# The MLP up projection of a two-block network with the high and low halves of the activations moved together, 512 columns per matmul

## The chip, the cores and the metric

One core of one Trainium2 chip. The metric is device microseconds of one launch, the median of several runs.

## The reference

A network of three layers on 256 tokens of width 1,024, all in float32. The first layer has sparse attention, forgetting attention and gated embeddings, the other two a mixer with cross attention, an output projection and an MLP. What the change touches is the MLP of the last two layers, cut to its lines:

```python
D_FF = 4 * D_MODEL          # 4,096

u = rms_norm(x, g_mlp[i])
x = x + jnp.square(jax.nn.relu(u @ w_ff1[i])) @ w_ff2[i]
```

`u` is 256 x 1,024, `w_ff1` 1,024 x 4,096 and `w_ff2` 4,096 x 1,024. So each MLP has an up projection, a squared relu, and a down projection that is added to `x`.

## The kernel before, in words

**Numbers.** Every float32 factor of a large product is split into a high part (rounded to the type float32r) and a low part (what is left, in the same type). A product then takes three matmuls that add up in PSUM: high by high, high by low, low by high. ScalarE makes the high part of a piece of weights (a copy with rounding from `raw` to `w_hi`, L677, in the loops of the MLP L954) and VectorE the low part (a subtraction into `w_lo`, L1024, in the loops L1349).

**Units.** Weights come in units of 128 x 2,048: four blocks of 128 rows by 512 columns. SyncE loads a unit into one of two landing buffers `raw` (L458), after waiting for the subtraction (`lo_ready`) of the unit that lay there. Split units lie in a ring of four slots; ScalarE and VectorE split three units ahead of TensorE. TensorE raises `unit_used` when it has used up a unit, and ScalarE waits for that before it writes a slot again. Every engine runs the same sequence of units, written out by hand, and signals the others by semaphores.

**The activations.** `u` is transposed on TensorE (L1506), and ScalarE and VectorE read the transposes from PSUM into `a_hi` (L693, L694) and `a_lo` (L1036), each 128 x 8 x 256: 8 blocks k of the width, 256 tokens.

**The MLP.** The hidden width of 4,096 is cut into FF = 8 chunks of 512. A chunk needs two up units (each four of the eight blocks k) and two down units (each 512 of the 1,024 output columns).

- Up (`up`, L1730 to L1744). The weights are stationary, 128 x 128 blocks (k, f) with f one of four parts of the chunk; the activations move, 256 columns. The result of part f is hidden-transposed, 128 x 256, in the first half of bank 4 + f. For each (k, f) there are three matmuls (L1742): w_hi with a_hi, w_hi with a_lo, w_lo with a_hi. A unit has 48 matmuls, a chunk 96.
- Eviction. ScalarE applies four relus, one per bank, from PSUM to `hidden` (L932, in the tile `tok`), each of which raises `ff_relu`. VectorE waits for all four and squares `hidden` in place (L1331). ScalarE rounds it to `b_hi` (L938), VectorE subtracts to `b_lo` (L1335) and raises `ff_lo`.
- Down (`product`, L1434 to L1450). The hidden values are stationary, the weights move, 512 columns: 24 matmuls for a unit, 48 for a chunk (L1446), which add up over all chunks in banks 0 to 3. The last unit of all goes by token tiles (L1460).

**The order on TensorE** (`mlp`, `chunk`). up(0), then for each chunk i: up(i+1), a wait for `ff_lo` of chunk i, down(i). Before the first matmul into bank f, up(i+1) waits until `ff_relu` says that this bank of chunk i was read (L1740). So chunk i+1 is evicted during down(i), except for chunk 0, whose eviction has no down product to lie beside: up(1) follows up(0) directly.

**The order on ScalarE in a chunk** (`chunk`, L946): split a unit, `hidden_hi`; split a unit, `hidden_relu` of the next chunk; split, split. `hidden_relu` waits for `unit_used` of the second up unit, `hidden_hi` also for the down product that read `b_hi` before. **On VectorE** (L1342): subtract for a unit, `hidden_lo`; subtract, `hidden_square`; subtract, subtract. What is queued behind a waiting instruction on an engine waits with it.

Of the kernel before, what the change touches and what calls it, by code (L numbers as in the profile page):

```python
# [18 lines left out]
ALU = mybir.AluOpType  # L19
ACT = mybir.ActivationFunctionType  # L20
AX = mybir.AxisListType
F32 = mybir.dt.float32
F32R = mybir.dt.float32r
BF16 = mybir.dt.bfloat16

P = 128
# [24 lines left out]
FF = 8  # L51
# [170 lines left out]
def build(nc, a, out):  # L222
    with ExitStack() as ctx:
        def sb(name, shape, dt=F32):
            return ctx.enter_context(nc.sbuf_tensor(name, shape, dt))

        def sem(name):
            return ctx.enter_context(nc.semaphore(name))
# [5 lines left out]
        tok = sb("tok", [P, NT, D])  # L234
        a_hi = sb("a_hi", [P, KT, S], F32R)
        a_lo = sb("a_lo", [P, KT, S], F32R)
        b_hi = sb("b_hi", [P, KT, S], F32R)
# [30 lines left out]

        bank = [ctx.enter_context(nc.psum_tensor(f"bank{i}", [P, 512], F32)) for i in range(8)]

        b_t, b_io, b_s, b_v, b_tr = bank[2], bank[3], bank[4:6], bank[7], bank[6:8]
        b_hid = bank[4:8]

        def group_bank(g):
# [60 lines left out]
        d_ready, y_ready, y_made = sem("d_ready"), sem("y_ready"), sem("y_made")  # L335
        ff_relu, ff_sq, ff_hi, ff_lo, rstd_sq = sem("ff_relu"), sem("ff_sq"), sem("ff_hi"), sem("ff_lo"), sem("rstd_sq")
        head_sum, ident_made = sem("head_sum"), sem("ident_made")
# [333 lines left out]
        def _(act):  # L671
# [253 lines left out]
            def mlp(base, lay, r, gx, gain):  # L925
                def hidden_relu(used, free):

                    act.wait_ge(unit_used, used)
                    if free is not None:
                        act.wait_ge(ff_lo, free)  # L930
                    for f in range(4):
                        act.activation(hidden[:, f, :], b_hid[f][:, 0:S], ACT.Relu).then_inc(ff_relu, 1)  # L932

# [9 lines left out]
                unit(base + 1)  # L943
                hidden_relu(base + 3, lay * FF if lay else None)

                def chunk(i, peeled):  # L946
                    for r_ in range(4):
# [10 lines left out]
                        if r_ == 1:  # L958
                            hidden_relu(i * 4 + (base + 5), i + (lay * FF + 1))
                with act.Fori(0, FF - 2) as i:  # L960
# [51 lines left out]
        def _(dve):  # L1012
# [315 lines left out]
            def mlp(base, lay, gx, gain):  # L1328
                def hidden_square(n):
                    dve.wait_ge(ff_relu, n * 4)  # L1330
                    dve.tensor_tensor(hidden, hidden, hidden, ALU.mult).then_inc(ff_sq, 1)  # L1331

# [100 lines left out]
        def _(pe):  # L1433
# [295 lines left out]
            def mlp(base, lay, gx, x_before, after):  # L1729
                def up(u, half_, slot, mid=(), read=None):  # L1730


                    pe.wait_ge(lo_ready, u + 1)
                    for k in range(4):
                        if k in mid:
                            mid[k]()
                        for f in range(4):
                            w = slice(k * CB + f * P, k * CB + f * P + P)
                            if read is not None and k == 0:
                                pe.wait_ge(ff_relu, read + (f + 1))  # L1740
                            for q, (wa, xa) in enumerate(((w_hi, a_hi), (w_hi, a_lo), (w_lo, a_hi))):
                                ins = pe.matmul(b_hid[f][:, 0:S], wa[:, slot, w], xa[:, 4 * half_ + k, :],  # L1742
                                                start=half_ + k + q == 0, stop=half_ == 1 and k == 3 and q == 2)
                    ins.then_inc(unit_used, 1)  # L1744
# [6 lines left out]
                def chunk(i, first, last):  # L1751

                    s = [(base + 2 + r) % RING for r in range(4)]
                    if not last:
                        up(i * 4 + (base + 2), 0, s[0], read=i * 4 + 4 * lay * FF)
                        up(i * 4 + (base + 3), 1, s[1])
# [116 lines left out]
```

## Time and profile before

| | |
|---|---|
| three runs | 882.53, 882.95, 885.64 us; median 882.95 |
| profiled execution, first to last instruction | 888.5 us (the page states no other time of it) |
| TensorE busy | 867.2 us, 4,726 matmuls |
| weight loads busy | 725.7 us, 4,726 loads |
| VectorE busy | 512.3 us |
| ScalarE busy | 420.8 us |
| mean granted TensorE clock | 0.987 of full speed |

PE is TensorE's matmuls and PEld its weight loads, which lie beside them; DVE is VectorE, ACT ScalarE, POOL GpSimd, SPq the queue of SyncE. L1742 is line 1742 of the kernel. Matmuls are pipelined: the duration shown of one (283 ns for 256 columns) is longer than the distance to the next, so their cost is read from the starts, or from the length of a stretch divided by its matmuls. In square brackets behind an instruction stand the idle time of its engine before it and what ended it. The MLP of the first of the two layers lies at 389 to 571 us of the span, that of the second at 704 to 885 us.

### The profile page before, as it was taken

The page shows a single profiled execution, that of the slowest core. Times are in us where ns is not written, and L with a number is a line of the kernel's source. Part 1 is how long each engine was busy: PE and PEld are TensorE (multiplying, and loading weights), DVE is VectorE, ACT ScalarE, POOL GpSimd, SP SyncE. Part 2 cuts the span into 40 slices and gives each one's busy share as a digit, 9 for nine tenths or more (in the row PEclk, how much of TensorE's full clock was granted, in tenths as well). Part 3 has the DMA queues.
Part 4 walks back from the last instruction along what each step waited for, and adds up shares of the span by engine and source line. Part 5 has one row for each costly group of instructions (what it writes and reads, how often), then busy time and mean ns, then how long its engine had stood idle before and what let it go on. Part 6 is the DMA issues. An engine that isn't in the chain of part 4 may idle for free. (4 is left out here: it accounts for less than half of the span.)

```text
span 888.5 us, 12248 instructions
## 1 busy us (share of the span) xinstructions
PE 867.2 (98%) x4726; PEld 725.7 (82%) x4726; DVE 512.3 (58%) x646; ACT 420.8 (47%) x613; POOL 132.3 (15%) x156
## 2 busy tenths in 40 slices
PE   7999999999999998999999999999999999999998
PEld 6996887777887775899999999877756899999996
DVE  5555576556767765455555555576764565555552
ACT  6445455454365554354444444445445454444440
POOL 3500010000003143002000000068940010000000
PEclk9998999999999998999999999999979999999999
DMA  8941234345655373146555555553310555555541
GB/s 321 299 142 37 68 123 142 98 140 174 206 200 186 133 243 122 42 149 201 183 189 188 187 188 189 188 190 99 139 48 18 172 190 190 189 189 189 188 142 48
DMA packets 76056, 140.59 MB, mean 158 GB/s; under 512 B 2728, under 2 KB 22384, under 8 KB 76016
## 3 DMA queue, kind: packets, MB, share of 16 engines
q1 hardware_dynamic: 73984, 134.03, 45.0%
q0 software_dynamic: 1872, 5.94, 2.1%
q8 instruction: 27, 0.44, 0.2%
q14 instruction: 13, 0.11, 0.0%
q10 hardware_dynamic: 160, 0.07, 0.0%
HBM read 138.99 MB, written 1.05 MB: 158 GB/s over the span
## 5 line engine op out<-in xcount | busy, mean ns | idle before, releaser
L1024 DVE TENSOR_TENSOR w_lo<-raw,w_hi 128x2048 fp32r<-128x2048 f32 (+2 forms) x69 | 157.7, 2287 | 76.3 <-ACT w_hi L677 75.6
L677 ACT ACTIVATE w_hi<-raw 128x2048 fp32r<-128x2048 f32 (+2 forms) x69 | 129.9, 1883 | 72.6 <-PE bank L1446 46.9
L1349 DVE TENSOR_TENSOR w_lo<-raw,w_hi 128x2048 fp32r<-128x2048 f32 x48 | 110.1, 2294 | 91.6 <-ACT w_hi L954 91.6
L1446 PE MATMUL bank<-w_hi,a_hi 128*128 128x512 f32 (+2 forms) x376 | 148.4, 395 | 0.4 <-PE bank L1446 0.4
L1446 PE MATMUL bank<-w_hi,b_hi 128*128 128x512 f32 x376 | 148.3, 394 | 0.3 <-DVE b_lo L1032 0.2
L1446 PE MATMUL bank<-w_lo,b_hi 128*128 128x512 f32 x376 | 146.6, 390 | 0.0
L1446 PE MATMUL bank<-w_hi,b_lo 128*128 128x512 f32 x376 | 146.5, 390 | 0.0
L1742 PE MATMUL bank<-a_hi,w_hi 128*128 128x256 f32 x512 | 145.3, 284 | 1.1 <-ACT tok L932 1.1
L1742 PE MATMUL bank<-a_lo,w_hi 128*128 128x256 f32 x512 | 144.9, 283 | 0.0
L1742 PE MATMUL bank<-a_hi,w_lo 128*128 128x256 f32 x512 | 144.9, 283 | 0.0
L1446 PE MATMUL bank<-w_lo,a_hi 128*128 128x512 f32 (+2 forms) x376 | 143.3, 381 | 0.0
L1446 PE MATMUL bank<-w_hi,a_lo 128*128 128x512 f32 (+2 forms) x376 | 143.3, 381 | 0.0
L954 ACT ACTIVATE w_hi<-raw 128x2048 fp32r<-128x2048 f32 x48 | 92.2, 1922 | 98.5 <-PE bank L1446 61.2
L1742 PEld LDWEIGHTS bank<-a_hi,w_hi 128*128 128x128 f32 x512 | 98.2, 192 | 2.0 <-DVE w_lo L1024 1.5
L1742 PEld LDWEIGHTS bank<-a_lo,w_hi 128*128 128x128 f32 x512 | 98.2, 192 | 0.5
L1742 PEld LDWEIGHTS bank<-a_hi,w_lo 128*128 128x128 f32 x512 | 98.2, 192 | 0.0
L1446 PEld LDWEIGHTS bank<-w_hi,a_hi 128*128 128x128 f32 x376 | 71.7, 191 | 15.0 <-issue 4.6
L1446 PEld LDWEIGHTS bank<-w_hi,b_hi 128*128 128x128 f32 x376 | 70.6, 188 | 15.1 <-issue 1.0
L1446 PEld LDWEIGHTS bank<-w_hi,b_lo 128*128 128x128 f32 x376 | 70.6, 188 | 15.1
L1446 PEld LDWEIGHTS bank<-w_lo,b_hi 128*128 128x128 f32 x376 | 70.7, 188 | 13.7
L1446 PEld LDWEIGHTS bank<-w_hi,a_lo 128*128 128x128 f32 x376 | 71.6, 190 | 11.7
L1446 PEld LDWEIGHTS bank<-w_lo,a_hi 128*128 128x128 f32 x376 | 71.8, 191 | 9.7
(213 smaller groups left out, 972.8 us busy)
## 6 DMA issues: line engine op xcount, KB each, us to landing
raw<-in_w_ff SPq DMA_DIRECT2D x64, 1024.0 KB, 5.1
raw<-in_w_out SPq DMA_DIRECT2D x12, 1024.0 KB, 5.0
raw<-in_w_in_moba SPq DMA_DIRECT2D x20, 512.0 KB, 4.4
raw<-in_w_merge SPq DMA_DIRECT2D x8, 1024.0 KB, 5.0
raw<-in_w_in SPq DMA_DIRECT2D x6, 880.0 KB, 7.5
m<-in_w_in SPq DMA_DIRECT2D x6, 880.0 KB, 6.9
raw<-in_w_mem_kv SPq DMA_DIRECT2D x4, 1024.0 KB, 5.2
raw<-in_w_ple_gate SPq DMA_DIRECT2D x4, 1024.0 KB, 5.0
```

Of the source, the lines that this page charges most:

```text
L677: act.activation(w_hi[:, slot, 0:n], landing[land][:, 0:n], ACT.Copy).then_inc(hi_ready, 1)
L954: act.activation(w_hi[:, (base + c) % RING, :], raw[:, (base + c) % RAW, :], ACT.Copy)\
L1024: dve.tensor_tensor(w_lo[:, v % RING, 0:n], landing[land_slot(v)][:, 0:n], w_hi[:, v % RING, 0:n].bitcast(F32), ALU.subtract).then_inc(lo_ ...
L1349: dve.tensor_tensor(w_lo[:, (base + c) % RING, :], raw[:, (base + c) % RAW, :], w_hi[:, (base + c) % RING, :].bitcast(F32), ALU.subtract). ...
L1446: ins = pe.matmul(banks[t][:, 0:n], xa[:, k0 + k, ts], wa[:, slot, w], start=first and k == 0 and q == 0, stop=last and k == kts - 1 and q ...
L1742: ins = pe.matmul(b_hid[f][:, 0:S], wa[:, slot, w], xa[:, 4 * half_ + k, :], start=half_ + k + q == 0, stop=half_ == 1 and k == 3 and q == 2)
```

## The change

`a_hi` and `a_lo` become two halves of one tile `a_both`, so that for a block k the 256 high and the 256 low columns lie side by side. Banks 4 to 7 become one PSUM tensor of four banks. For each (k, f) the up projection moves all 512 columns past w_hi in one matmul: the first half of the bank gets w_hi by a_hi, the second w_hi by a_lo. A second matmul of 256 columns adds w_lo by a_hi to the first half. So there are two matmuls in place of three, 64 for a chunk in place of 96. In the last block k the short one comes first, so that the long one closes the group.

The eviction sums the two halves: ScalarE copies the second halves of all four banks to `hidden` in one instruction of 1,024 columns, in place of four relus (`ff_part` replaces `ff_relu`); VectorE adds the first halves of the banks to it (1,024 columns, raises `ff_sum`), and then takes max(h, 0) * h in one instruction in place of the square. TensorE waits once for `ff_sum`, ahead of the first matmul of an up stretch, in place of four times for `ff_relu`.

```diff
--- before.py
+++ after.py
@@ -232,8 +232,8 @@
         w_lo = sb("w_lo", [P, RING, UNIT], F32R)
         x = sb("x", [P, NT, D])
         tok = sb("tok", [P, NT, D])
-        a_hi = sb("a_hi", [P, KT, S], F32R)
-        a_lo = sb("a_lo", [P, KT, S], F32R)
+        a_both = sb("a_both", [P, KT, 2, S], F32R)
+        a_hi, a_lo = a_both[:, :, 0, :], a_both[:, :, 1, :]
         b_hi = sb("b_hi", [P, KT, S], F32R)
         b_lo = sb("b_lo", [P, KT, S], F32R)
         proj = sb("proj", [P, NT * DIN])
@@ -266,10 +266,13 @@
         hstat = sb("hstat", [P, N_NORMED, 2, NT * 4])
         half = sb("half", [P, NT * 4])
 
-        bank = [ctx.enter_context(nc.psum_tensor(f"bank{i}", [P, 512], F32)) for i in range(8)]
+        low = [ctx.enter_context(nc.psum_tensor(f"bank{i}", [P, 512], F32)) for i in range(4)]
+        high = ctx.enter_context(nc.psum_tensor("bank4", [P, 4, 512], F32))
+        bank = [b[:, :] for b in low] + [high[:, i, :] for i in range(4)]
 
         b_t, b_io, b_s, b_v, b_tr = bank[2], bank[3], bank[4:6], bank[7], bank[6:8]
         b_hid = bank[4:8]
+        hid_lo, hid_hi = high[:, :, 0:S], high[:, :, S:2 * S]
 
         def group_bank(g):
 
@@ -333,7 +336,8 @@
         merge_sig, merged, x_post, z_made = sem("merge_sig"), sem("merged"), sem("x_post"), sem("z_made")
         ple_block, d_copied_a, d_copied_v = sem("ple_block"), sem("d_copied_a"), sem("d_copied_v")
         d_ready, y_ready, y_made = sem("d_ready"), sem("y_ready"), sem("y_made")
-        ff_relu, ff_sq, ff_hi, ff_lo, rstd_sq = sem("ff_relu"), sem("ff_sq"), sem("ff_hi"), sem("ff_lo"), sem("rstd_sq")
+        ff_part, ff_sum = sem("ff_part"), sem("ff_sum")
+        ff_sq, ff_hi, ff_lo, rstd_sq = sem("ff_sq"), sem("ff_hi"), sem("ff_lo"), sem("rstd_sq")
         head_sum, ident_made = sem("head_sum"), sem("ident_made")
         act_chain, vec_chain, pool_chain = sem("act_chain"), sem("vec_chain"), sem("pool_chain")
 
@@ -923,13 +927,12 @@
             evac(B_KV0)
 
             def mlp(base, lay, r, gx, gain):
-                def hidden_relu(used, free):
+                def hidden_part(used, free):
 
                     act.wait_ge(unit_used, used)
                     if free is not None:
                         act.wait_ge(ff_lo, free)
-                    for f in range(4):
-                        act.activation(hidden[:, f, :], b_hid[f][:, 0:S], ACT.Relu).then_inc(ff_relu, 1)
+                    act.activation(hidden, hid_hi, ACT.Copy).then_inc(ff_part, 1)
 
                 def hidden_hi(n, used, k=0):
 
@@ -941,7 +944,7 @@
                 groups(gx, 2, a_hi, gain)
                 x_squares(r, X_OUT0 + 2 if lay == 0 else X_OUT1 + 2, m_hi)
                 unit(base + 1)
-                hidden_relu(base + 3, lay * FF if lay else None)
+                hidden_part(base + 3, lay * FF if lay else None)
 
                 def chunk(i, peeled):
                     for r_ in range(4):
@@ -956,7 +959,7 @@
                         if r_ == 0:
                             hidden_hi(i + (lay * FF + 1), i * 4 + (base + 3))
                         if r_ == 1:
-                            hidden_relu(i * 4 + (base + 5), i + (lay * FF + 1))
+                            hidden_part(i * 4 + (base + 5), i + (lay * FF + 1))
                 with act.Fori(0, FF - 2) as i:
                     chunk(i, False)
                 chunk(FF - 2, True)
@@ -1327,8 +1330,10 @@
 
             def mlp(base, lay, gx, gain):
                 def hidden_square(n):
-                    dve.wait_ge(ff_relu, n * 4)
-                    dve.tensor_tensor(hidden, hidden, hidden, ALU.mult).then_inc(ff_sq, 1)
+                    dve.wait_ge(ff_part, n)
+                    dve.tensor_tensor(hidden, hid_lo, hidden, ALU.add).then_inc(ff_sum, 1)
+                    dve.wait_ge(ff_sum, n)
+                    dve.scalar_tensor_tensor(hidden, hidden, 0.0, hidden, ALU.max, ALU.mult).then_inc(ff_sq, 1)
 
                 def hidden_lo(n, k=0):
                     dve.wait_ge(ff_hi, n)
@@ -1731,16 +1736,20 @@
 
 
                     pe.wait_ge(lo_ready, u + 1)
+                    if read is not None:
+                        pe.wait_ge(ff_sum, read)
                     for k in range(4):
                         if k in mid:
                             mid[k]()
+                        kt = 4 * half_ + k
+                        x_both = a_both[:, kt].rearrange("p q n -> p (q n)")
                         for f in range(4):
                             w = slice(k * CB + f * P, k * CB + f * P + P)
-                            if read is not None and k == 0:
-                                pe.wait_ge(ff_relu, read + (f + 1))
-                            for q, (wa, xa) in enumerate(((w_hi, a_hi), (w_hi, a_lo), (w_lo, a_hi))):
-                                ins = pe.matmul(b_hid[f][:, 0:S], wa[:, slot, w], xa[:, 4 * half_ + k, :],
-                                                start=half_ + k + q == 0, stop=half_ == 1 and k == 3 and q == 2)
+                            if kt < KT - 1:
+                                pe.matmul(b_hid[f], w_hi[:, slot, w], x_both, start=kt == 0, stop=False)
+                            ins = pe.matmul(b_hid[f][:, 0:S], w_lo[:, slot, w], a_hi[:, kt, :], start=False, stop=False)
+                            if kt == KT - 1:
+                                ins = pe.matmul(b_hid[f], w_hi[:, slot, w], x_both, start=False, stop=True)
                     ins.then_inc(unit_used, 1)
                 mids = upper(gx, x, x_half, x_before + 2)
 
@@ -1752,7 +1761,7 @@
 
                     s = [(base + 2 + r) % RING for r in range(4)]
                     if not last:
-                        up(i * 4 + (base + 2), 0, s[0], read=i * 4 + 4 * lay * FF)
+                        up(i * 4 + (base + 2), 0, s[0], read=i + (lay * FF + 1))
                         up(i * 4 + (base + 3), 1, s[1])
                     pe.wait_ge(ff_lo, i + (lay * FF + 1))
                     for c in range(2):
```

## Rows read from the trace of the kernel before

**Rows 1.** The page: busy time of each engine
```profile
PE 867.2 (98%) x4726; PEld 725.7 (82%) x4726; DVE 512.3 (58%) x646; ACT 420.8 (47%) x613; POOL 132.3 (15%) x156
```

**Rows 2.** The chain that ended last, in order of time: start us, us, what
```profile
...
739.84 11.51 PE bank L1742 x96
751.35 10.91 PE bank L1446 x48
...
```

**Rows 3.** One chunk by windows: length; busy PE, PEld, DVE, ACT, POOL; PEclk, DMA, GB/s
```profile
739.84:751.35 11.51, 11.51 (x98) 11.51 (x97) 5.72 (x3) 4.78 (x3) 0.00 (x0) 1.00 0.60 185
751.35:762.26 10.91, 10.91 (x51) 9.02 (x50) 5.81 (x3) 4.93 (x6) 0.00 (x0) 1.00 0.56 191
```

**Rows 4.** Timeline of PE, end of the first up stretch, layer 1: start, us
```profile
...
716.34 0.28 PE L1742 MATMUL bank<-a_hi,w_lo 128*128 128x256 f32 x1
717.18 0.36 PE L1742 MATMUL bank<-a_hi,w_hi 128*128 128x256 f32 x1 [0.56 <-ACT tok L932]
...
```

**Rows 5.** Timeline of PE, the same place in layer 0
```profile
...
402.44 0.36 PE L1742 MATMUL bank<-a_hi,w_hi 128*128 128x256 f32 x1 [0.56 <-ACT tok L932]
...
```

**Rows 6.** The chain of waits inside the first up stretch: transposes, and the wait
```profile
...
707.11 0.44 PE bank L1506 x4
717.05 0.14 issue
...
```

**Rows 7.** Timeline of ACT, then of DVE, at the first eviction of layer 1
```profile
...
716.65 1.21 ACT L932 ACTIVATE tok<-bank 128x256 f32<-128x256 f32 x4 [2.47 <-PE bank L1742]
...
714.21 2.29 DVE L1024 TENSOR_TENSOR w_lo<-raw,w_hi 128x2048 fp32r<-128x2048 f32 x1 [0.81 <-ACT w_hi L677]
717.90 1.23 DVE L1331 TENSOR_TENSOR tok<-tok 128x1024 f32<-128x1024 f32 x1 [1.39 <-ACT tok L932]
...
```

**Rows 8.** Groups of instructions by line and shape, ACT: count, busy us, mean ns, idle before
```profile
...
L932 ACT ACTIVATE tok<-bank 128x256 f32<-128x256 f32 x64 | 19.4, 389 | 58.7 <-PE bank L1742 58.7
L938 ACT ACTIVATE b_hi<-tok 128x1024 fp32r<-128x1024 f32 x16 | 16.7, 1044 | 0.0
L690 ACT ACTIVATE a_hi<-bank 128x512 fp32r<-128x512 f32 x9 | 5.4, 598 | 7.9 <-PE bank L1506 7.8
...
```

**Rows 9.** The same view for DVE
```profile
...
L1331 DVE TENSOR_TENSOR tok<-tok 128x1024 f32<-128x1024 f32 x16 | 19.6, 1226 | 41.4 <-ACT tok L932 41.4
L1032 DVE TENSOR_TENSOR a_lo<-bank,a_hi 128x512 fp32r<-128x512 f32 x9 | 6.2, 689 | 4.4 <-ACT a_hi L690 4.4
L1290 DVE SCALAR_TENSOR_TENSOR m<-m 128x1024 f32<-128x1024 f32 x2 | 2.5, 1226 | 2.4 <-ACT m L897 2.4
...
```

**Rows 10.** Timeline of ACT, then of DVE, from the second eviction on
```profile
...
728.97 1.21 ACT L932 ACTIVATE tok<-bank 128x256 f32<-128x256 f32 x4 [3.85 <-PE bank L1742]
...
730.22 1.23 DVE L1331 TENSOR_TENSOR tok<-tok 128x1024 f32<-128x1024 f32 x1 [2.77 <-ACT tok L932]
732.01 2.29 DVE L1349 TENSOR_TENSOR w_lo<-raw,w_hi 128x2048 fp32r<-128x2048 f32 x1 [0.57 <-ACT w_hi L954]
744.04 1.22 DVE L1335 TENSOR_TENSOR b_lo<-tok,b_hi 128x1024 fp32r<-128x1024 f32 x1
...
```

**Rows 11.** Timeline of DVE in the last chunk of layer 1
```profile
...
868.75 1.22 DVE L1335 TENSOR_TENSOR b_lo<-tok,b_hi 128x1024 fp32r<-128x1024 f32 x1
...
```

**Rows 12.** Timeline of PE: its three longest idle times after the start-up
```profile
...
337.08 0.66 PE L1567 MATMUL bank<-ident,proj 128*128 128x128 f32 x2 [4.63 <-POOL proj L598]
...
596.22 0.41 PE L1567 MATMUL bank<-ident,proj 128*128 128x128 f32 x2 [1.19 <-POOL proj L598]
...
655.25 0.55 PE L1633 MATMUL bank<-ident,prob 128*128 128x128 f32 x3 [1.20 <-DVE prob L1166]
...
```

**Rows 13.** Busy time by window after these idle times; PEclk is the granted clock
```profile
336.00:342.60 6.60, 5.52 (x15) 4.43 (x16) 2.29 (x1) 2.03 (x3) 5.55 (x6) 0.50 0.71 233
596.00:600.00 4.00, 3.78 (x17) 2.86 (x17) 3.10 (x5) 0.80 (x3) 3.67 (x5) 1.00 0.52 174
657.00:662.00 5.00, 5.00 (x16) 2.68 (x15) 1.63 (x8) 2.46 (x10) 0.00 (x0) 0.50 0.02 3
```

## The prediction

> **What bounds the kernel now.** I read the page first. TensorE is busy for 98% of the span, VectorE for 58%, ScalarE for 47% [rows 1]. A busy share alone proves nothing, so I next read the chain that ended last. In one chunk of an MLP it is TensorE alone: 96 up-projection matmuls of 256 columns in 11.51 us, then 48 down-projection matmuls of 512 columns in 10.91 us, and no other engine between them [rows 2]. The windows of the same chunk show the granted clock at 1.00, so the full 2.4 GHz, while DVE works 5.7 of 11.5 us [rows 3]. So in the steady part only TensorE's own issue sets the time. There is one exception in each layer: after the very first up stretch nothing can be put between it and the next one, as the first down product needs the hidden values of a chunk already finished. There TensorE idles until a bank has been read. In layer 1 the last matmul starts at 716.34 and the next at 717.18 [rows 4]; layer 0 shows the same 0.56 us of idle time [rows 5].
>
> **Term 1, the matmuls.** For each weight block (k, f) the change replaces three 256-column matmuls by one of 512 and one of 256. Their spacing is 11.51 / 96 = 119.9 ns and 10.91 / 48 = 227.3 ns [rows 2]. Before: 3 x 119.9 = 359.7 ns. After: 227.3 + 119.9 = 347.2 ns. The columns moved are the same 768; what goes is one of three fixed parts. At 2.4 GHz 256 columns are 106.7 ns and 512 are 213.3 ns, so 13.2 and 14.0 ns of each spacing are not columns. 32 blocks x 8 chunks x 2 layers = 512 blocks, so 512 x 12.5 ns = **6.4 us less**, all on the path. The rounding of the two stretches (0.01 us each) is 0.2 us of this. The 512-column matmul is priced by the down projection, whose moving operand is as long and as contiguous as the new one, but the trace has no alternation of the two sizes. Bounds for the block: above, 359.7 ns, no gain; below, 227.3 + 106.7 = 334.0 ns, the short matmul paying for its columns alone. I take 347.2, since the fixed part has nearly the same size in both stretches.
>
> A rule speaks against this term. The Trainium skill (TensorE: Matmul & The Clock Gate, Back-to-back issue gap) gives warm matmuls N / 2.4 + 2.5 ns apart. By that, each matmul saved is worth 2.5 ns, term 1 is 1.3 us, and the total comes out slower than before. The trace disagrees with the rule by some 11 ns at either size, and I follow the trace.
>
> **Term 2, the first eviction of each layer.** Before, the second up stretch waited bank by bank for ff_relu, so the first of four relus released it. Now one wait on ff_sum covers all four banks, and that needs ScalarE's copy of all high halves and, behind it, VectorE's add. Let N be the moment at which the next matmul would start without a wait. Before, N = 716.34 + 0.12 = 716.46; the first relu starts at 716.65, 0.19 after N [rows 4, 7], takes 0.39, and TensorE starts 0.14 after it [rows 6]: N + 0.72. After: 0.19, then a copy of 1,024 columns. ScalarE takes 389 ns for 256 columns and 598 for 512 [rows 8], so 209 ns per 256 more, 1.02 us for 1,024; the 1,024-column copy from SBUF took 1.04. I take 1.03. Then 0.04 to VectorE (717.86 to 717.90 would be the same step), an add of 1.23 as for 1,024 columns from SBUF [rows 9], and 0.14: N + 2.63. So 1.91 us more in each layer, **3.8 us more** in all. Upper bounds, if a strided read over four banks cost as its parts: copy 4 x 389 = 1.56, add 2 x 689 = 1.38 [rows 8, 9], 0.68 more in each layer, 5.2 in all. Below I see no way under 3.7: both are serial. VectorE is free in time; its weight subtraction ended at 716.50 [rows 7].
>
> **Everything later is covered.** In the steady part the eviction starts when the up stretch ends (728.97) and is needed at 739.84, after a down stretch. Copy to 730.0 (shorter than the four relus' 1.21), add to 731.3: 8.5 us to spare. The added instruction is the second on VectorE: max and square in one, 1.23 us as its like [rows 9], to 732.5. Queued behind it is the weight subtraction that now starts at 732.01 [rows 10], and behind that SP's next load, which waits for the subtraction; both come about 0.5 us later. Their own weights are needed a chunk half later. The hidden low half ends at 744.04 + 1.22 = 745.3, needed at 751.35: 6 us spare. At the end of layer 1 it ends at 869.97 [rows 11] and is needed when 48 matmuls from 863.3 on are over, at 874.2: 4.2 us spare against 1.3 more. ScalarE gets shorter: one copy in place of four relus, 1.03 for 1.21, with the weight roundings queued behind it. If this cover were gone, each of 16 chunks would pay what is over. The new layout of a_hi and a_lo changes only strides between runs of 256; I cost it at nothing, its writers having idle time before them (7.9 us on ScalarE's [rows 8]). No DMA is added or moved.
>
> **Sum.** -6.4 + 3.8 = **-2.6 us**. Each term is a difference inside one profiled execution. The page gives only its span, 888.5 us, and that stands 5.5 us above the median of the three runs, 882.95; I apply the difference to the median: 880.35. With the bounds of the two terms the forecast's own range is -2.9 to -1.0 us, and the three runs shown scatter by -0.4 to +2.7.
>
> **Rival 1, the clock falls at the longer wait (ends slower).** The idle time shown would go from 0.56 to 0.56 + 1.91 = 2.5 us. Two idles of 1.2 us lie far below that [rows 12]: after one, the clock stayed at 1.00, after the other, in a stretch of small matmuls, it fell to 0.50, which is 1.2 GHz. At the idle of 4.63 us it also fell, for the 6.6 us shown [rows 12, 13]. Our 2.5 us lies between, and dense 2.4 GHz work on both sides speaks against a fall. From the point at which 2.5 us is enough, one fall costs up to half of 6.6 us, 3.3: -2.6 + 3.3 = +0.7, 883.6 us; in both layers +4.0, 887.0.
>
> **Rival 2, no cheaper block.** The fixed part of 13 ns isn't paid per matmul when sizes alternate; a block takes 359.7 ns as before. Then only term 2 is left: +3.8, 886.8 us. Against it: two streams with the same fixed part although one has twice the columns. The skill's rule above is nearest to this case.
>
> **Rival 3, weight loads were the limit.** Loads are busy for all of the up stretch, 11.51 of 11.51 us, against 9.02 of 10.91 in the down stretch [rows 3]. If the 119.9 ns are a load's and not the matmul's, and a load can go ahead during the 512-column matmul, the block takes 334.0 ns: 512 x 25.7 = 13.2 us less, -9.4 in all, 873.6 us. Against it: four 128-column transposes with their loads pass in 0.44 us [rows 6], 110 ns each, so a load alone isn't longer than that; and a load would have to run two matmuls ahead.
>
> **How the numbers follow.** Forecast 0.58, rival 1 0.25, rival 2 0.07, rival 3 0.07, the rest (above all an eviction that comes late in every chunk) 0.03. About what a measurement can tell from no change is 0.5%, 4.4 us. Faster by more: rival 3 and 0.03 of the forecast, 0.10. Slower by more: two falls with term 2 at its upper bound 0.03, rival 2 with a longer wait or a fall 0.04, the rest 0.02, so 0.09. Within: 0.81. The range runs from 877.5 (the forecast's best, 880.0, less scatter of the runs and some of the way to rival 3) to 886.0 (past one fall, with scatter); it leaves out rival 3, rival 2 and two falls, under 2 in 10.
>
> **What would show it.** Right: an up stretch of 64 matmuls in 11.1 us; one idle of 2.5 us per layer before the second up stretch, released by VectorE's add; the new add near 1.23 us; the clock at 1.00 in the 7 us after it; no wait of TensorE elsewhere in the MLPs; one weight load fewer per block. Wrong: an up stretch of 11.5 or of 10.7 us (rivals 2 and 3), 0.50 in the clock column after the wait (rival 1), or waits of TensorE for b_lo or ff_sum in each chunk.

## The result, and the profile after

| | before | changed |
|---|---|---|
| median, 20 executions each | 885.83 us | 891.41 us |
| lowest, highest | 882.53, 898.03 | 885.50, 902.09 |
| ratio, 95% interval | 1 | 1.0057, 1.0029 to 1.0085 |
| profiled execution: time, span, mean clock | span 888.5, clock 0.987 | 886.73, 884.9, 0.990 |

The ratio compares undisturbed executions; those more than 1.5% above the fastest of their kernel are left out of it, and with them most of those that lost most to the clock. The change makes the kernel about 0.6% slower; measured twice more (e5_again, e11_third below) the same kernel was 0.3 and 0.2% slower, with intervals that reach 1. Over all 44 executions of it and 121 of before the mean time is 4.0 us longer, 0.45%. The forecast was 880.35 us, 2.6 below the median of three runs then shown; 891.41 lies outside the range of 877.5 to 886.0. The median of before has itself risen by 2.9 us with more executions.

The pages first. The changed kernel has a third less up-projection matmuls, 448 + 512 + 64 in place of 1,536, and still the chain that ended last is TensorE's.

```profile
PE 860.6 (97%) x4214; PEld 697.6 (79%) x4214; DVE 530.5 (60%) x662; ACT 417.8 (47%) x565; POOL 130.6 (15%) x156
...
PE 31%; DVE 1%; POOL 1%; ACT 0%; issue 0%
...
L1749 PE MATMUL bank<-a_both,w_hi 128*128 128x512 f32 x448 | 160.7, 402 | 4.9 <-DVE tok L1334 4.9
...
L935 ACT ACTIVATE tok<-bank 128x1024 f32<-128x1024 f32 x16 | 16.4, 1026 | 56.6 <-PE bank L1752 56.6
L1334 DVE TENSOR_TENSOR tok<-bank,tok 128x1024 f32<-128x1024 f32 x16 | 19.6, 1225 | 36.4 <-ACT tok L935 36.4
```

The copy of 1,024 columns takes 1.03 us and the add 1.23, as in the forecast. Now a steady up stretch by windows, and the stretch right behind the wait of the second MLP (columns as in [rows 3]), both of the changed kernel:

```profile
737.48:748.77 11.29, 11.29 (x65) 9.81 (x64) 5.72 (x3) 4.79 (x3) 0.00 (x0) 1.00 0.61 187
```

```profile
715.39:726.56 11.17, 11.17 (x64) 9.79 (x65) 6.83 (x4) 4.70 (x3) 0.00 (x0) 1.00 0.51 173
```

An up stretch took 11.51 us before [rows 2, 3]. It takes 11.29 now, 0.22 less, and the forecast was 0.40 less. All twelve steady stretches show 11.29 or 11.30. Only the one behind the second wait comes near the forecast, at 11.17 or 11.18.

The waits of the two MLPs, from the timeline of PE in the changed kernel:

```profile
403.46 0.77 PE L1749 MATMUL bank<-a_both,w_hi 128*128 128x512 f32 x1 [2.46 <-DVE tok L1334]
404.02 0.41 PE L1750 MATMUL bank<-a_both,w_lo 128*128 128x256 f32 x1
...
715.39 0.47 PE L1749 MATMUL bank<-a_both,w_hi 128*128 128x512 f32 x1 [2.46 <-DVE tok L1334]
715.70 0.28 PE L1750 MATMUL bank<-a_both,w_lo 128*128 128x256 f32 x1
```

Both are 2.46 us, where 0.56 stood before [rows 4, 5]. But the matmuls behind the first take 0.77 and 0.41 us, behind the second 0.47 and 0.28. The windows tell why; PEclk is the granted clock:

```profile
396.00:403.20 7.20, 4.99 (x29) 4.07 (x27) 5.32 (x3) 3.71 (x4) 6.08 (x14) 1.00 0.52 164
403.20:406.60 3.40, 3.14 (x10) 2.69 (x11) 2.87 (x3) 2.86 (x2) 2.21 (x6) 0.50 0.76 279
406.60:413.00 6.40, 6.40 (x38) 5.55 (x37) 2.35 (x3) 1.92 (x1) 0.00 (x0) 1.00 0.51 164
```

The clock fell from 2.4 to 1.2 GHz at the end of the first wait, for 3.4 us. That is rival 1. In dense work half of 3.4 us is 1.7 us; read from the starts, the stretch behind this wait took 12.78 us and the one behind the second, at full clock, 11.18. The question is whether it explains a loss of 5 us.

**How the executions are compared.** Every execution comes with its span and its mean granted clock c. I call (1 - c) x span the part lost to the clock; where an expectation below speaks of the time without the clock's part, it subtracts this whole. Over all executions of all kernels here a straight line fits with a residual of 1.0 us: time = T + 0.83 x part lost, with a T for each kernel (why the slope is below 1 was not looked into). T is the time at full clock. Both are used below.

### The profile page after: what moved, and what is told of

It is laid out like the page before. It is cut to its first block and busy times, and to the rows that moved or that the text cites. A ratio compares the mean times of both kernels' runs of the same rounds, so it can differ in the third digit from the quotient of the medians.

```text
span 884.9 us, 11144 instructions
## 1 busy us (share of the span) xinstructions
PE 860.6 (97%) x4214; PEld 697.6 (79%) x4214; DVE 530.5 (60%) x662; ACT 417.8 (47%) x565; POOL 130.6 (15%) x156
## 5 line engine op out<-in xcount | busy, mean ns | idle before, releaser
L1451 PE MATMUL bank<-w_hi,a_both 128*128 128x512 f32 (+2 forms) x752 | 239.3, 389 | 0.4 <-PE bank L1451 0.4
L1749 PE MATMUL bank<-a_both,w_hi 128*128 128x512 f32 x448 | 160.7, 402 | 4.9 <-DVE tok L1334 4.9
L1451 PEld LDWEIGHTS bank<-w_hi,a_both 128*128 128x128 f32 x752 | 142.9, 191 | 26.6 <-issue 4.6
L1451 PE MATMUL bank<-w_lo,a_both 128*128 128x512 f32 (+2 forms) x376 | 143.5, 382 | 0.0
L1750 PE MATMUL bank<-a_both,w_lo 128*128 128x256 f32 x512 | 141.6, 282 | 0.0
L1749 PEld LDWEIGHTS bank<-a_both,w_hi 128*128 128x128 f32 x448 | 84.9, 189 | 26.2 <-issue 5.5
L1750 PEld LDWEIGHTS bank<-a_both,w_lo 128*128 128x128 f32 x512 | 97.4, 190 | 1.3
L1451 PEld LDWEIGHTS bank<-w_lo,a_both 128*128 128x128 f32 x376 | 72.0, 192 | 9.6
L1334 DVE TENSOR_TENSOR tok<-bank,tok 128x1024 f32<-128x1024 f32 x16 | 19.6, 1225 | 36.4 <-ACT tok L935 36.4
L792 ACT ACTIVATE probT<-bank 128x384 f32<-128x384 f32 (+1 forms) x36 | 18.5, 514 | 46.1 <-PE bank L1638 45.9
```

The source lines that it names most:

```text
L792: act.activation(probT[:, h % 2, 0:n], b_t[:, 0:n], ACT.Copy).then_inc(pt_copied, 1)
L1334: dve.tensor_tensor(hidden, hid_lo, hidden, ALU.add).then_inc(ff_sum, 1)
L1451: ins = pe.matmul(banks[t][:, 0:n], xa[:, k0 + k, ts], wa[:, slot, w], start=first and k == 0 and q == 0, stop=last and k == kts - 1 and q ...
L1749: pe.matmul(b_hid[f], w_hi[:, slot, w], x_both, start=kt == 0, stop=False)
L1750: ins = pe.matmul(b_hid[f][:, 0:S], w_lo[:, slot, w], a_hi[:, kt, :], start=False, stop=False)
```

## The experiments

Fourteen runs. This table has them all; T has an error of 0.2 us for the first two lines and of 0.3 to 0.4 for the others. The mean part lost has an error of 0.5 us for before, 1.1 for the changed kernel, 1.2 for e1_fill, 0.3 for e8_before_early and 1.3 to 2.8 for the rest. "Large" counts the executions that lost 13 us or more to the clock. The ratio of the second line is that of the 20 executions above.

| kernel | median us | ratio to before, 95% | T | mean part lost | large |
|---|---|---|---|---|---|
| before | 885.9 | | 879.0 | 10.7 | 27 of 121 |
| changed, with e5 and e11 | 891.4 | 1.0057 (1.0029 to 1.0085) | 878.9 | 15.7 | 25 of 44 |
| e1_fill, both waits filled | 885.29 | 0.999 (0.9969 to 1.001) | 878.7 | 9.1 | 1 of 13 |
| e9_fill0, the first filled | 887.33 | 1.0004 (0.9985 to 1.0023) | 878.9 | 11.2 | 2 of 13 |
| e10_fill1, the second filled | 897.09 | 1.0043 (1.0 to 1.0087) | 879.1 | 17.1 | 7 of 12 |
| e13_shift | 887.13 | 1.0004 (0.9971 to 1.0038) | 880.0 | 11.9 | 4 of 13 |
| e4_before_late | 892.34 | 1.0052 (1.0019 to 1.0084) | 883.0 | 13.6 | 4 of 13 |
| e14_before_shift | 889.06 | 1.0001 (0.996 to 1.0041) | 880.8 | 14.4 | 5 of 12 |
| e2_bank | 883.38 | 0.9982 (0.9949 to 1.0015) | 876.2 | 13.0 | 4 of 12 |
| e3_early | 879.85 | 0.9912 (0.9874 to 0.9951) | 874.2 | 11.4 | 3 of 10 |
| e7_early2 | 881.11 | 0.9928 (0.9892 to 0.9963) | 873.5 | 12.2 | 4 of 14 |
| e12_best | 880.50 | 0.9926 (0.9897 to 0.9955) | 873.1 | 10.5 | 1 of 7 |
| e8_before_early | 883.84 | 0.9983 (0.9961 to 1.0005) | 877.5 | 6.9 | 0 of 12 |
| e6_grouped | 887.18 | 1.0013 (0.9986 to 1.004) | 877.9 | 11.9 | 3 of 12 |

The first two lines alone answer most of it. T is the same: 878.9 against 879.0. What the matmuls gain, the waits take. The changed kernel loses 5.0 us more to the clock (error 1.2), and 0.83 x 5.0 = 4.1 us is the difference of the mean times, 891.9 and 887.9.

**Fill the waits.**

```diff
                 up(base + 1, 1, (base + 1) % RING, mids[1])
+                for _ in range(10):
+                    pe.matmul(bank[3], a_both[:, 0, 0, 0:P], a_both[:, 0].rearrange("p q n -> p (q n)"), start=True, stop=True)
```

> The changed kernel, with ten 512-column matmuls into an unused bank placed in the wait between the first and the second up stretch of each layer (10 x 0.227 = 2.3 us of the 2.5 us idle). Theory A (the longer idle makes the clock fall, in layer 0 at this wait in the trace of after, and that is where the loss is): no stretch at clock 0.50 in the 10 us behind this place in either layer, second up stretch 11.2 to 11.3 us, and the time comes back to that of before, ratio 0.998 to 1.002. Theory B (the falls of the clock are chance and have nothing to do with the wait; the loss is the wait itself and dearer blocks): nothing changes against the changed kernel, ratio about 1.006.

Idle is down to 0.18 us and the second stretch starts no earlier:

```profile
400.49 2.45 PE L1760 MATMUL bank<-a_both 128*128 128x512 f32 x10
403.12 0.47 PE L1749 MATMUL bank<-a_both,w_hi 128*128 128x512 f32 x1 [0.18 <-DVE tok L1334]
```

The windows of the 10 us behind it, and behind the second wait of the same kernel, are at clock 1.00:

```profile
403.00:413.00 10.00, 9.88 (x56) 8.60 (x57) 6.87 (x4) 4.72 (x3) 2.11 (x6) 1.00 0.58 198
725.00:735.00 10.00, 9.82 (x56) 8.48 (x56) 6.73 (x5) 4.78 (x3) 0.00 (x0) 1.00 0.58 199
```

T does not move (878.7), the part lost falls from 15.7 to 9.1 us, and the ratio is 0.999, as theory A had it. Useless work in the wait makes the kernel faster. So the idle time of TensorE, and not the length of the wait, is what costs beyond T.

The two stretches behind the filled waits were not both 11.2 to 11.3 us long, as expected:

```profile
403.12:414.48 11.36, 11.36 (x64) 9.89 (x65) 7.05 (x4) 4.60 (x3) 1.99 (x5) 1.00 0.50 172
725.34:736.52 11.18, 11.18 (x65) 9.80 (x65) 6.84 (x4) 4.61 (x3) 0.00 (x0) 1.00 0.49 170
```

Both come after 0.18 us of idle, in the same order of matmuls at the same clock. So the short stretch of 11.17 us in the changed kernel isn't owed to the length of the idle before it.

**The wait alone, in the kernel before.**

```diff
+                    if read is not None:
+                        pe.wait_ge(ff_sq, read)
...
-                            if read is not None and k == 0:
-                                pe.wait_ge(ff_relu, read + (f + 1))
...
-                        up(i * 4 + (base + 2), 0, s[0], read=i * 4 + 4 * lay * FF)
+                        up(i * 4 + (base + 2), 0, s[0], read=i + (lay * FF + 1))
```

> The kernel before with one edit: an up stretch waits for the square of the chunk (ff_sq) and not for the relu of the bank. All matmuls are as before; the first wait of each layer gets as long as in the changed kernel (0.19 + 1.21 + 0.04 + 1.23 + 0.14 = 2.8 us, 2.1 more than before), elsewhere it is covered by the down stretch. Theory A: +4.2 us of wait, and the clock falls to 0.50 behind it in some executions for 1.7 to 3.4 us more each: ratio 1.006 to 1.011. Theory B: +4.2 us alone, ratio 1.0048, clock at 1.00 behind both waits.

T is 4.0 us above that of before, where 4.2 was expected. The idle is 2.65 us at both places, and the profile shows the clock at 0.50 behind it at 404.3 and again at 728.6:

```profile
402.90:404.30 1.40, 1.40 (x12) 1.40 (x13) 0.00 (x0) 1.40 (x2) 1.40 (x8) 1.00 1.03 399
404.30:407.70 3.40, 3.40 (x18) 3.40 (x18) 3.35 (x2) 0.97 (x2) 0.20 (x1) 0.50 0.15 56
407.70:413.00 5.30, 5.30 (x46) 5.30 (x46) 0.78 (x2) 1.91 (x1) 0.00 (x0) 1.00 0.63 198
...
728.60:732.00 3.40, 3.40 (x17) 3.40 (x17) 1.92 (x1) 2.40 (x2) 0.00 (x0) 0.50 0.52 202
```

The fall needs none of the new matmuls. At the first wait it came 1.4 us after TensorE had begun to work again, so it need not lie in the idle time but can follow it. The part lost is 2.9 us more than before, with an error of 2.0. The ratio, 1.0052, is just below what was expected of theory A (1.006 to 1.011) and cannot be told from B by itself; the two falls in the trace decide for A.

**The changed kernel again.** Twice, once as the reference of the fills of one wait.

> The changed kernel itself once more, beside the kernels of this call. So far, time less what the clock took ((1 - mean clock) x span, for each execution) is 877.2 us for before and 876.1 for the changed kernel, while the part lost to the clock is 8.8 us (median) before and 15.1 after. Theory A: this holds again; the time without the clock's part is 0.5 to 1.5 us below that of before, the part lost is 3 to 6 us larger, and a profile shows a fall behind one or both of the 2.5 us waits. Theory B (the clock's part was the chance of that session): the clock's part is within 1.5 us of that of before, and the ratio is 0.998 to 1.000.

It measured 890.33 us, ratio 1.0029 (0.9996 to 1.0062), part lost 15.9 us. The fall at 403.1 us is there again, none behind the second wait.

> The changed kernel a third time, as the reference for the two beside it in the same call: time without the clock's part as before (within 0.5 us), mean loss 14 to 17 us, large losses in a third to two thirds of the executions; one more profile, in which the fall behind the first wait should be there, and either one behind the second or a long one near 650 us.

It measured 892.68 us, ratio 1.0024 (0.999 to 1.0059), part lost 15.5 us, large in 7 of 12. Its profiled execution lost 17.4 us, a large loss. It has three falls to look at: behind the first wait, in the attention of the last mixer, and behind the second wait.

```profile
402.10:405.50 3.40, 3.40 (x11) 2.92 (x12) 2.89 (x2) 2.60 (x2) 1.92 (x5) 0.50 0.67 249
...
654.70:668.40 13.70, 13.61 (x41) 7.40 (x41) 5.21 (x21) 5.43 (x19) 1.37 (x2) 0.50 0.00 0
...
719.50:722.90 3.40, 3.12 (x9) 2.67 (x10) 2.64 (x3) 2.86 (x2) 0.00 (x0) 0.50 0.71 267
```

**Which wait?** Two kernels with the filling matmuls in one MLP only; e9_fill0 has the condition shown, e10_fill1 has `U_FF1` in it.

```diff
-                for _ in range(10):
+                for _ in range(10 if base == U_FF0 else 0):
```

> The changed kernel with the ten filling matmuls in the wait of the first MLP only (at 400 us); the wait of the second (at 713 us) stays idle. So far the part lost to the clock is 15.8 us (mean of 32 executions) in the changed kernel, 9.1 with both waits filled, 10.4 before, and losses of 13 us and more are in 18 of 32 executions of the changed kernel, 1 of 13 filled. Theory A1 (each wait only costs its own fall, 1.7 us apiece): mean loss 13 to 14, large losses as often as in the changed kernel. Theory A2 (the fall at the first wait also makes the falls at 580 to 685 us longer, by what it does to the timing ahead of them): mean loss 9.5 to 12 here, large losses in at most 3 of 12.

> The same with the second wait filled and the first idle. Theory A1: mean loss 13 to 14. Theory A2: as in the changed kernel less the second wait's own fall, mean 14 to 16, large losses in a third to a half of the executions, and a profile shows the fall at 403 us.

The two kernels do the same work, T 878.9 and 879.1, and both leave one wait of 2.46 us idle. With the first filled the part lost is 11.2 us and large in 2 of 13; with the second filled 17.1 and large in 7 of 12. This speaks for A2, in two small samples: an idle first wait brings more than its own fall. Before lost 10.4 to 11.9 us on average on each of four chips, so the chip doesn't explain the difference.

What is a large loss made of? Six profiled executions lost more than 20 us (e1, e2, e4, e7, e9, e13), and each has one stretch of 30.7 or 34.1 us at 1.2 GHz in the small matmuls of the attention, from 651 to 657 us on. In the profile of e9_fill0, one of its two executions with such a loss, it is this:

```profile
653.90:688.00 34.10, 34.10 (x103) 18.22 (x102) 12.37 (x50) 12.75 (x44) 1.14 (x2) 0.50 0.00 0
```

The kernel before has a shorter one at the same place, 10.2 us in its profile with 11.9 us lost. But 13 us are also passed without a long stretch, and more easily by a kernel with falls at its waits: e11_third reached 17.4 us with 13.7 us there and two falls of 3.4, and the profile of e6_grouped 13.7 us with none there, but falls at both waits and one at 599 us. So "large" counts two things. At 20 us the changed kernel has 12 of 44 executions and before 21 of 121, which chance can give. If the line for before is lowered by two falls, from 13 to 9.6 us, it has 39 of 121 against the 25 of 44, and chance hardly gives that. e9_fill0 and e10_fill1 keep their 2 of 13 and 7 of 12 at 20 us.

In e10_fill1 the profile showed no fall at 403 us after the same 2.46 us, so the fall doesn't come each time, against what was expected of that profile.

**Does the shift do it?** A fall at the first wait moves everything behind it by 1.7 us. Two kernels make that shift without a fall: 17 filling matmuls in place of 10 in the first wait, and eleven in the kernel before. The first edit is that of e13_shift, on top of e1_fill, the second that of e14_before_shift, at the same place of the kernel before.

```diff
-                for _ in range(10):
+                for _ in range(17 if base == U_FF0 else 10):
...
+                for _ in range(11 if base == U_FF0 else 0):
+                    pe.matmul(bank[3][:, :], a_hi[:, 0, 0:P], a_hi[:, 0:2, :].rearrange("p k n -> p (k n)"), start=True, stop=True)
```

> The changed kernel with both first waits filled, the first by 17 matmuls in place of 10: 7 x 0.227 = 1.6 us more at full clock, about what a fall of the clock there costs, and no fall. Time without the clock's part: 0.3 us of the 1.6 is still the wait, so 1.2 us above e1_fill. If the shift of everything behind by 1.6 us makes the later falls long, losses of 13 us and more come in a third to two thirds of the executions and the mean loss is 13 to 17 us. If it does not, they come in at most 3 of 12, mean 9 to 11.

> The kernel before with eleven 512-column matmuls into an unused bank after the first up stretch of the first MLP: 2.5 us, of which 0.7 cover the wait there, so +1.8 us without the clock's part. If the shift makes the later falls long: mean loss 13 to 17 us, ratio to before above 1.005. If not: mean loss 9 to 11 as before, ratio 1.001 to 1.003.

T rose by 1.3 and 1.8 us, as expected. Large losses came in 4 of 13 and 5 of 12, 9 of 25 together. That lies between the 27 of 121 of before and the 32 of 56 of the changed kernel and e10_fill1 together. It decides nothing. Nor is the idle first wait the whole rule: e4_before_late and e6_grouped have it too and show 4 of 13 and 3 of 12. All kernels with it make 39 of 81, those with the wait filled or at most 1.02 us (before and its shift among them, e1, e2, e3, e7, e8, e9, e12, e13) 51 of 227. At 20 us these are 23 of 81 and 44 of 227, which no longer tells them apart.

**Where the matmuls' gain went.** The blocks (k, f) in another order: all four 512-column matmuls of a row k, then all four of 256.

```diff
-                        for f in range(4):
...
-                            if kt < KT - 1:
-                                pe.matmul(b_hid[f], w_hi[:, slot, w], x_both, start=kt == 0, stop=False)
-                            ins = pe.matmul(b_hid[f][:, 0:S], w_lo[:, slot, w], a_hi[:, kt, :], start=False, stop=False)
+                        if kt < KT - 1:
+                            for f in range(4):
+                                pe.matmul(b_hid[f], w_hi[:, slot, ws[f]], x_both, start=kt == 0, stop=False)
+                        for f in range(4):
+                            ins = pe.matmul(b_hid[f][:, 0:S], w_lo[:, slot, ws[f]], a_hi[:, kt, :], start=False, stop=False)
...
```

> The changed kernel with the matmuls of a block row k in another order: four of 512 columns, then four of 256, so that sizes alternate once in eight matmuls. Steady up stretches of the changed kernel take 11.29 us and not the 11.11 of the forecast. If the alternation of sizes costs the missing 5.6 ns per block, the stretch is 11.11 to 11.15 us here and the time without the clock's part 2 to 3 us lower than that of the changed kernel. If it is something else (a 512-column matmul of this shape is dearer than one of the down projection), it stays at 11.29. Waits and the clock's part as in the changed kernel either way.

The steady stretch by windows:

```profile
428.30:439.51 11.21, 11.21 (x66) 9.83 (x65) 5.72 (x3) 4.78 (x3) 0.00 (x0) 1.00 0.58 189
```

11.21 us, 0.08 of the missing 0.18. T is 1.0 lower (error 0.4), not 2 to 3. So the alternation of sizes is a part of it and not all. The expectation was right in kind and too large.

**Take the wait away.** First the eviction bank by bank, as before the change.

```diff
-                    act.activation(hidden, hid_hi, ACT.Copy).then_inc(ff_part, 1)
+                    for f in range(4):
+                        act.activation(hidden[:, f, :], hid_hi[:, f, :], ACT.Copy).then_inc(ff_part, 1)
...
-                    dve.wait_ge(ff_part, n)
-                    dve.tensor_tensor(hidden, hid_lo, hidden, ALU.add).then_inc(ff_sum, 1)
-                    dve.wait_ge(ff_sum, n)
+                    for f in range(4):
+                        dve.wait_ge(ff_part, n * 4 + (f - 3))
+                        dve.tensor_tensor(hidden[:, f, :], hid_lo[:, f, :], hidden[:, f, :], ALU.add).then_inc(ff_sum, 1)
+                    dve.wait_ge(ff_sum, n * 4)
...
-                    if read is not None:
-                        pe.wait_ge(ff_sum, read)
...
+                            if read is not None and k == 0:
+                                pe.wait_ge(ff_sum, read * 4 + (f - 3))
```

> The changed kernel with the eviction bank by bank: four copies of 256 columns, four adds of 256, TensorE waits for ff_sum of one bank. The wait should end 0.19 + 0.39 + 0.04 + 0.42 + 0.14 = 1.2 us after the next matmul could start, in place of 2.7. Theory A: 2 x 1.5 = 3 us less from the wait, and no fall of the clock there, so ratio to before 0.995 to 0.999. Theory B: only the 3 us less than the changed kernel, ratio about 1.0025.

The idle is 1.02 us, T 876.2: 2.7 us below the changed kernel, for 3 expected. The median part lost is 7.9 us and its profile has no fall at either wait. Its mean is 13.0, from four executions of large loss, so these come without a wait of 2.46 us too.

Then, on top of e2_bank, the second up unit in an order that finishes bank 0 early; ScalarE copies a bank as soon as `ff_bank` says that it is finished:

```diff
+                    for k in range(2 if half_ else 4):
...
+                        for f in range(4):
+                            ins = block(k, f)
+                    if half_:
...
+                        for f in range(4):
+                            block(2, f)
+                            ins = block(3, f)
+                            if f < 3:
+                                ins.then_inc(ff_bank, 1)
```

> As the one before, and the second up unit finishes bank by bank (blocks k = 2 and 3 of bank f together), so that bank 0 can be evicted 2 us before the stretch ends. No idle of TensorE at the first eviction (before: 0.56 us). Theory A and B both: 12 to 14 steady chunks x 0.22 us less plus twice the 0.7 us that before waits, so 4 to 5 us less than before at the same clock. A: ratio 0.993 to 0.997. B: the clock falls as in the changed kernel by chance, ratio 0.997 to 1.002.

0.9912: faster than before beyond the interval. T is 4.8 us under it, as expected, though an idle of 0.52 us remained, since VectorE's weight subtraction lay ahead of the adds. So the next kernel takes the adds first:

```diff
                 unit(base)
-                unit(base + 1)
                 hidden_square(lay * FF + 1)
+                unit(base + 1)
```

> The third kernel of the first call (bank-wise eviction, second up unit finished bank by bank) with one more edit: VectorE does the first adds of a layer before its second weight subtraction, which held them up to 399.87 there. The first adds then start near 398.3, and the 0.52 us idle before the second up stretch goes in both layers: 1.0 to 1.5 us less than e3_early without the clock's part (872.3), so 871; ratio to before 0.989 to 0.993 by either theory.

The 0.52 us of idle are gone. T is 0.7 lower with an error of 0.5, where 1.0 to 1.5 was expected, and the ratio cannot be told from that of e3_early. To see how much of this is the order and how much the wide matmuls, the kernel before got the same order, with its relus:

> The kernel before, its matmuls of 256 columns kept, with the second up unit finished bank by bank so that relus run during the stretch. What e3_early gains over before is then split: the idle of 0.56 us goes here too, 2 x 0.7 = 1.4 us less than before without the clock's part (877.2), so 875.8. If this kernel came as low as e3_early (872.3), the 512-column matmuls would have no part in that gain; by the traces they have 3.5 us of it.

T 877.5, 1.5 under before (1.4 expected), ratio 0.9983. It lost least of all to the clock, 6.9 us with no large loss in 12; but the three kernels with this order and the wide matmuls have 8 large losses in 31, so this isn't shown to be the order's doing. Of the 5.5 us of e7_early2 this leaves 4.0 for the wide matmuls, where 12 steady and 4 first stretches of 0.22 to 0.25 us give 3.5 to 4.0. At last both orders together:

> A version meant to beat both: e7_early2 (bank-wise eviction, second up unit finished bank by bank, first adds ahead of the weight subtraction) with the order of e6_grouped where a block row runs over all banks. e7_early2 stands 5.5 us under before without the clock's part; the grouped rows cover 6 of 8 block rows of a stretch whose gain was 0.08 us, so 12 x 0.06 = 0.7 us more. Ratio to before 0.990 to 0.994, no idle over 0.2 us at the first eviction.

Timeline of PE behind the first eviction of the second MLP, and a steady stretch by windows, of e12_best:

```profile
708.37 0.50 PE L1751 MATMUL bank<-a_both,w_hi 128*128 128x512 f32 x1 [0.20 <-DVE tok L1339]
```

```profile
730.06:741.24 11.18, 11.18 (x65) 9.79 (x65) 7.04 (x5) 5.94 (x6) 0.00 (x0) 1.00 0.69 228
```

0.9926 (0.9897 to 0.9955), 5.9 us under before at full clock. It beats both kernels; it cannot be told from e3_early and e7_early2 by its ratio.

## Why the prediction was wrong

Two steps of it failed: the clock was put at nothing in the sum, and it took some 4 us of time more; and term 1 was sized at 6.4 us, and it is 3.5 to 3.9. A third part of the miss is the starting point. Of the 11.1 us between the forecast, 880.35, and the median measured, 2.9 are the starting point, some 2.5 term 1 and some 4.1 the clock by the means; the rest, about 1.5, is that the medians differ by 5.6 us where the means differ by 4.0.

- **What bounds the kernel.** Right. TensorE alone, in both kernels; no wait for b_lo or ff_sum in a steady chunk, in any trace.
- **Term 1, -6.4 us.** The mechanism held, the size was off. A block takes 11.29 / 32 = 352.8 ns and not 347.2: 6.9 ns less than before and not 12.5, so 512 x 6.9 = 3.5 us. The step that failed is "the 512-column matmul is priced by the down projection". e6_grouped shows that alternating sizes has a part in it (0.08 of 0.18 us). That the stretch behind the wait takes 11.17 us with the same order was not explained by any run. The stretches behind the filled waits of e1_fill, 11.36 and 11.18 us at the same idle, show only that the length of the idle isn't the reason. The text called the lack of such an alternation in the trace by name, and its bounds for the block, 334.0 to 359.7 ns, held the value. But the stated range of -2.9 to -1.0 us left these bounds out: it took only the rounding, 0.2 us, for term 1. With 359.7 ns its upper end is +5.2 and not -1.0.
- **The rule against term 1.** The Trainium skill (TensorE: Matmul & The Clock Gate, Back-to-back issue gap) gives 2.5 ns beyond N / 2.4 for each warm matmul, by which term 1 would be an estimated 1.3 us. The trace of after gives 3.5, between the rule and the forecast. The section calls this the gap of an isolated matmul, and for a stream of pairs of weight load and matmul it gives some 131 ns at N = 512; the 227.3 ns of the down stretch here disagree with that by far more.
- **Term 2, +3.8 us.** Right to 0.1: the idle is 2.46 us, forecast 2.5, the copy 1.03, the add 1.23; e4_before_late, which adds 2 x 2.1 us of wait, moved T by 4.0.
- **Everything later is covered.** Right.
- **Sum without the clock.** With term 1 at its measured size, -3.5 + 3.8 = +0.3. The fit gives -0.1 with an error of 0.3. So the true price of the work was nothing, where -2.6 was forecast. The trace of layer 1 says the same. From the first up matmul to the first steady stretch, both kernels at full clock, first before and then changed:

```profile
704.08:739.68 35.60, 35.03 (x250) 32.97 (x248) 20.29 (x15) 18.39 (x23) 3.94 (x3) 1.00 0.53 178
700.61:737.48 36.87, 34.41 (x185) 29.40 (x184) 22.64 (x17) 18.03 (x17) 3.94 (x3) 1.00 0.50 171
```

  That is 1.27 us more, with 1.90 us more of wait in it, and six steady stretches of 0.22 us less are -1.3. So the two first stretches of the layer give 0.6 us and not 0.4, and term 1 is nearer 3.9 us.
- **Rival 1, held at 0.25.** This is the larger step that failed: the sum puts the clock at nothing. "Dense 2.4 GHz work on both sides speaks against a fall" was wrong: all three profiles of the changed kernel have the fall at the first wait, one of them at the second too, and so has the kernel before with the wait made longer. Its price was read too high for one fall (3.4 us at half clock, 1.7 lost, where 3.3 was the bound) and too low in all: the part lost rose by 5.0 us (error 1.2), more than two falls of 1.7. Falls were seen at four of the six waits in its three profiles, which is 2.3 us an execution and about half of the 5.0. What is left was not seen directly. The counts of large losses, 25 of 44 against 27 of 121, are in part the two falls themselves, which push a middling loss past 13 us; with the line for before lowered by them it is 25 of 44 against 39 of 121, so something beyond them does come more often. Stretches near 654 us are the candidate: e11_third has one of 13.7 us there, and e9_fill0 against e10_fill1 (2 of 13, 7 of 12) points to the first wait; e4_before_late and e6_grouped, with the same wait and few large losses, speak against it. Whether and how a fall at 403 us does this 250 us later stays open; the test of the mere shift fell between the two answers.
- **The starting point.** The forecast was put on a median of three runs, 882.95. Single executions of before lose 5 to 24 us to the clock, so three of them place it poorly: the median of 20 was 885.83.
- **The chances.** Same within 0.5% had 0.81; the measured 0.57% has an interval that spans 0.5%, and the two repeats gave 0.3 and 0.2%. That the total came within 0.5% or near it is no merit of the sum, whose sign was wrong.

## What to carry to other kernels

The price of a wait of TensorE isn't its length. Once it is some 2.5 us long in the middle of dense work, it can cost a fall of the clock behind it, and an eviction that was split by bank should stay split if anything waits for its first bank. Where a wait can't be avoided, see first whether the work ahead can be ordered so that the first bank is done early; that made a gain of 0.7% of a change that had lost 0.2 to 0.6%. And compare executions by their granted clock: a fit of the time against the part lost to the clock told differences of 1 us from scatter of 20. Count rare losses with more than one threshold before building on the count.

## What the runs showed of the hardware

- An idle of TensorE of 2.46 to 2.65 us between dense stretches was followed by 3.4 us at 1.2 GHz in 8 of the 12 places seen in the profiles of the changed kernel, e4, e6, e9 and e10; idles of 1.02 us and less at these places were not, in the nine other profiles and the two filled waits of e9 and e10. In two of them the fall came 1.4 and 1.3 us after the work had begun again (e4_before_late at its first wait, e6_grouped at its second).
- In float32r with 128-column weight loads between, 512-column matmuls stand 227.3 ns apart alone and some 232 ns in rows of four, and a pair of 512 and 256 columns takes 352.8 ns in steady alternation. The stretch behind the wait gives 349 or 355 ns a pair (11.17 and 11.36 us), at idles of 0.18 us too.
- Without any change the same kernel's executions spread from 881 to 901 us, and nearly all of it is the granted clock: the fit leaves a residual of 1.0 us.
